# One hybrid block in float32 precision: topk rounds, score evictions and filler matmuls of the first mixer put in another order

## What is computed

```
proj = h @ w_in[l]
(c_q, k_a, v_a, k_idx, w_idx, q_b, k_b, v_b, gate_a, gate_b) = jnp.split(proj, offsets, axis=-1)
...
y_a = dsa_attention(q_a, k_a, v_a, q_idx, k_idx, w_idx, w_uv_a[l], top_k)      # 128 best keys by an index score
y_b = stick_breaking_attention(q_b, k_b, v_b)                                  # 8 heads of 64, causal
merged = jax.nn.sigmoid(gate_a) * (y_a @ w_o_a[l]) + jax.nn.sigmoid(gate_b) * (y_b @ w_o_b[l])
x = x + merged @ w_out[l]
```

## Time and profile before

| | us |
|---|---|
| median of 3 runs | 1981.68 (1981.31 to 1981.76) |
| the profiled execution | 1981.31 |
| its span, first to last instruction | 1979.4 |
| TensorE busy | 1901.5 (96%) |
| VectorE busy | 1044.2 (53%) |
| ScalarE busy | 699.4 (35%) |
| mean granted clock | 0.992 |

### The profile page before, as it was taken

One profiled execution on the slowest core, in us unless ns is written; L12 is line 12 of the kernel. 1 busy time (PEld: TensorE's weight loads), 2 busy tenths in 40 slices (PEclk: granted clock), 3 DMA queues, 4 the chain that ended last, 5 costly groups with the idle time before them and its releaser, 6 DMA issues.

```text
span 1979.4 us, 21957 instructions
## 1 busy us (share of the span) xinstructions
PE 1901.5 (96%) x8807; PEld 1373.9 (69%) x8807; DVE 1044.2 (53%) x1690; ACT 699.4 (35%) x1139; POOL 42.0 (2%) x67
## 2 busy tenths in 40 slices
PE   7999999998999989999999999999999999999998
PEld 6888888875888757888888878877676444443443
DVE  5443554457887886544334447566765333332333
ACT  5321232335655364333222234565642111111111
POOL 0000000100000001000000000000001000000000
PEclk9999999999999999999999999999999999999999
DMA  6323334125333304333333323222169999999997
GB/s 174 101 88 99 103 96 107 52 76 62 81 84 63 103 22 149 91 94 100 89 106 96 96 86 98 73 64 64 58 246 374 421 420 420 420 421 420 420 421 286
DMA packets 256302, 338.65 MB, mean 171 GB/s; under 512 B 10001, under 2 KB 218897, under 8 KB 232641
## 3 DMA queue, kind: packets, MB, share of 16 engines
q1 hardware_dynamic: 249744, 320.71, 47.2%
q0 software_dynamic: 5872, 15.41, 2.2%
q10 hardware_dynamic: 576, 1.05, 0.1%
HBM read 332.74 MB, written 8.39 MB: 172 GB/s over the span
## 4 chain that ended last, share of the span: by engine, by line
PE 71%; DMA 11%; DVE 10%; ACT 6%; issue 2%; SPq 0%; DVEq 0%; ACTq 0%
PE bank L183 70%; DMA large<-w_up 10%; PE bank L186 1%; ACT wH L189 1%; ACT T L189 1%; ACT p L189 1%; DVE PTL L195 1%; DVE y L195 1%; DVE p L198 1%; DVE score L201 0%; ACT SPH L189 0%; DVE st L207 0%; DVE gt L195 0%; DVE stage4L L195 0%; DMA gates<-gt 0%
## 5 line engine op out<-in xcount | busy, mean ns | idle before, releaser
L183 PE MATMUL bank<-hH,wH 128*128 128x512 f32 x1096 | 432.6, 395 | 12.4 <-DVE stage0L L195 11.7
L183 PE MATMUL bank<-hL,wH 128*128 128x512 f32 x1096 | 427.3, 390 | 0.0
L189 ACT ACTIVATE wH<-stage 128x1024 fp32r<-128x1024 f32 (+3 forms) x231 | 228.5, 999 | 98.3 <-PE bank L183 84.0
L183 PE MATMUL bank<-large,xF 128*64 128x512 f32 x1024 | 237.8, 607 | 17.2 <-DMA large<-w_up 15.1
L183 PEld LDWEIGHTS bank<-hH,wH 128*128 128x128 f32 x1096 | 206.3, 188 | 58.0 <-DVE stage0L L195 11.7
L183 PEld LDWEIGHTS bank<-hL,wH 128*128 128x128 f32 x1096 | 206.3, 188 | 43.5 <-issue 1.7
L183 PEld LDWEIGHTS bank<-large,xF 128*64 128x64 f32 x1024 | 75.6, 139 | 149.6 <-issue 142.2
L183 PE MATMUL bank<-hidH,wH 128*128 128x512 f32 x352 | 137.4, 390 | 2.1 <-DVE stage2L L195 0.9
L183 PE MATMUL bank<-hidL,wH 128*128 128x512 f32 x352 | 136.9, 389 | 0.0
L195 DVE TENSOR_TENSOR yoL<-bank,yoH 64x512 fp32r<-64x512 f32 x64 | 44.1, 689 | 148.7 <-ACT yoH L189 147.7
L183 PE MATMUL bank<-large,hF 128*64 128x512 f32 x512 | 116.0, 595 | 0.0
(11 more groups left out here) (494 smaller groups left out, 3339.6 us busy)
## 6 DMA issues: line engine op xcount, KB each, us to landing
large<-w_gate SPq DMA_DIRECT2D x64, 1024.0 KB, 27.0
large<-w_up SPq DMA_DIRECT2D x64, 1024.0 KB, 26.7
large<-w_down SPq DMA_DIRECT2D x64, 1024.0 KB, 26.7
stage<-w_in SPq DMA_DIRECT2D x56, 512.0 KB, 4.1
stage<-w_gate SPq DMA_DIRECT2D x44, 512.0 KB, 3.8
stage<-w_up SPq DMA_DIRECT2D x44, 512.0 KB, 3.8
stage<-w_down SPq DMA_DIRECT2D x16, 512.0 KB, 3.5
stage<-w_out SPq DMA_DIRECT2D x12, 512.0 KB, 3.9
```

The lines of the kernel that those rows point to most:

```text
L183: return self.e.matmul(*a, **k) if self.e is not None else Nothing()
L189: return self.e.activation(*a, **k) if self.e is not None else Nothing()
```

## The change

It does four things.

1. In the list of steps, rounds of `topk` stand at other places within the same section between two even `b1`, the number per section being the same. In the section before `b1(0)` two rounds are now ahead of the evictions of the pair's projections. Before `b1(2)` two rounds and a third are ahead of the evictions and of `b1_split(1)`, with a fourth behind that. Before `b1(4)` the eviction of `gate(7)` waits for a later `evict()`, two rounds stand ahead of `b1_max(3)`, and `b1_split(3)` is behind the evictions. Before `b1(6)` `b3(4)` and its eviction are earlier, and a round stands ahead of the evictions.
2. `b1` of an even head waits for the remainder of both halves of the keys (`kb_even` and `kb_oddL`) and no longer for the even half alone.
3. Filler matmuls: 9 ahead of `b1(0)`, 7 ahead of `b1(2)`, 9 ahead of `b1(6)`, and 13 where there were 6 ahead of `expand(0)`.
4. `values(0)` stands behind `logits(4)` and the eviction of a gate.

```diff
-                left.append(Step("split_qk", ..., y=gts.take(("qk_odd", c) if which else ("qk", c)), ...
+                left.append(Step("split_qk", ..., y=gts.take(("qk", c, which)), ...
...
             score(3, 1, low4)
+            topk(1)
             qk(0, 1, 7)
+            topk(1)
             evict()
+            topk(1)
+            gate(5)
             topk(2)
-            gate(5)
-            topk(3)
             b1(0)
...
             qk(3, 0, 6)
+            b3(4)
             qk(3, 1, 7)
+            b3_split(4)
             part("b1_max", 5)
...
-            values(0)
             logits(4)
             evict()
+            values(0)
             topk(2)
             expand(0)
...
-                        keep_clock(s.banks[0], {0: 6}.get(n, 0))
+                        keep_clock(s.banks[0], {0: 13}.get(n, 0))
...
                     elif s.kind == "b1":
+                        keep_clock(s.z[0], {0: 9, 2: 7, 6: 9}.get(n, 0))
                         pe.wait_ge(*after("kb_zero", n % 2))
-                        pe.wait_ge(*after("qk_odd" if n % 2 else "qk_even", n // 2))
-                        pe.wait_ge(*after("qk", n // 2))
+                        pe.wait_ge(*after("qk", n // 2, 1))
...
-                            low(M.qb[1][:, :], s.y.t[:, :], M.qb[0][:, :], 0.125).then_inc(*did("qk", n))
+                            low(M.qb[1][:, :], s.y.t[:, :], M.qb[0][:, :], 0.125).then_inc(*did("qk", n, 0))
...
-                                low(M.kb[e][1][pp, :], s.y.t[pp, :], M.kb[e][0][pp, :]).then_inc(*did(("qk_even", "qk_odd")[e], n))
+                                t = low(M.kb[e][1][pp, :], s.y.t[pp, :], M.kb[e][0][pp, :])
+                            t.then_inc(*did("qk", n, 1))
```

More of the change, by code:

```diff
@@ L546, in qk @@
                 b = dense(steps, ("qk", c, which), wcols("w_in", (520, 1032)[which] + c * 128, 128), 8, h, ("qkf", c, which), None, n)
-                left.append(Step("split_qk", n=c, k=which, bank=b, y=gts.take(("qk_odd", c) if which else ("qk", c)), held=("mm", "b1", 2 * c - 1) if c else ("sc", 3, 7)))
+                left.append(Step("split_qk", n=c, k=which, bank=b, y=gts.take(("qk", c, which)), held=("mm", "b1", 2 * c - 1) if c else ("sc", 3, 7)))
             def vb_rows(kk):
@@ L679, in mixer1 @@
             part("b1_max", 1)
+            topk(2)
+            evict()
             topk(1)
             part("b1_split", 1)
-            evict()
             b3(0)
+            topk(1)
+            qk(1, 1, 7)
             b3_split(0)
-            qk(1, 1, 7)
             evict()
             part("b2", 1)
-            topk(4)
+            topk(1)
             part("b2_exp", 1)
@@ L710, in mixer1 @@
             b3(2)
+            topk(2)
             part("b1_max", 3)
-            topk(1)
-            part("b1_split", 3)
             evict()
             b3_split(2)
+            part("b1_split", 3)
+            topk(1)
             qk(2, 1, 7)
+            part("b2", 3)
+            topk(1)
             evict()
-            part("b2", 3)
-            topk(3)
             part("b2_exp", 3)
@@ L744, in mixer1 @@
             part("b1_split", 5)
+            topk(1)
             evict()
-            b3(4)
-            b3_split(4)
             part("b2_exp", 5)
-            topk(2)
+            topk(1)
             part("b2_split", 5)
```

## The result

The kernel with the change took 1993.1 us (median of 5 runs, 1992.2 to 1994.95); the kernel before took 1981.76 on the same chip (1981.31 to 1985.2). The ratio is 1.0056, with a 95% interval of 1.0045 to 1.0068. The forecast was 1991.8, the direction slower. The profiled execution of after took 1993.76, with a span of 1991.9, so the span is 12.5 longer than before's 1979.4.

What follows compares the result with a forecast made beforehand. TensorE works nearly without a break, its even b1 mostly released by VectorE's kb_even, so work ahead of that counts. Terms 2.30 + 2.72 + 4.78 - 0.1 + 0.4 = 10.1 us gave 1991.8, range 1985.5 to 1995.5.

Steps and rivals of the forecast that it cites:

- b1(0): First even b1: starts at 500.83 against 498.39, 2.44 us late, 1.72 for two rounds and 0.72 for the wait.
- small slack of 0.14: At b2(0), which had waited 0.14 us for VectorE: lateness behind it is 2.44 - 0.14 = 2.30 us.
- b2(1) and b1(2): Second section: b2(1) newly waits 1.5 us for T1L; b1(2) starts at 539.10, 5.02 us late, 2.72 more.
- b1(4): Third section: 3.8 us wait for bank 7, covered by later keys on VectorE; start 581.26, 9.80 late, 4.78 more.
- the rival in which the clock falls: Clock falls in the unfilled holes at qk(2,1) and b1(4), 1.5 us longer or more: 1993.3 to 1994.8, chance 0.16.
- a sign of being wrong: PEclk below 1 between 560 and 585 with b1(4) at its forecast start; then the time is higher.
- b1(6): Last even b1: starts 1.44 us later on kb_oddL, held clock gives back 1.5; sum -0.1, start near 620.9.
- expand(0): Starts at about 687.0 against 684.43, mostly former idle; transposes at 687.8, fillers remove the half-speed stretch; +0.4 us.
- The sum: All five terms, b1(0) to expand(0): 10.1 us, nothing behind gives it back; time 1991.8.
- part of the delay is not on the path: Moved rounds fit VectorE's 3.40 us hole, b1(4) term about half, 2.4 less, b2(1)'s 1.5 absorbed: 1988, chance 0.12.
- absorbed later: Expert stage streams weights; if its start did not hang on PE, all would end as before, 1982; chance 0.05.
- Faster by the clock: Fillers keep the clock full from b1(6) and expand(0) on, VectorE waits do not grow: 1978.5, chance 0.05.

Runs made afterwards that it cites:

- first section alone: Kernel before with only the first section's topk rounds moved, two ahead of the evictions of the first pair: 1987.25 us, ratio 1.0019.
- wait alone: Kernel before with one change, b1 of an even head waiting for the remainder of both halves of the keys: 1987.99 us, ratio 1.0029.
- gate 7's eviction back: Kernel after with the eviction of gate 7 put back to behind b2(2), everything else as after: 1993.66 us, ratio 1.0048.
- second profile of before: Kernel before, unchanged, profiled a second time: 1984.11 us in one run, beside 1984.33 for before.
- the kernel with the edits at expand: Kernel before with values(0) behind logits(4) and the gate's eviction, and 13 fillers ahead of expand(0): 1982.38 us in one run, beside 1983.13 for before.
- the fillers alone: Kernel before with only the filler matmuls, 9, 7 and 9 ahead of b1(0), b1(2), b1(6) and 13 for 6 ahead of expand(0): 1984.85 us, ratio 1.0015.
- third section alone: Kernel before with only the third section's order, gate 7's later eviction and the moved rounds, neither the wait nor fillers: 1987.79 us, ratio 1.0018.
- gate 7 late alone: Kernel before with only the eviction of gate 7 made late, no topk round moved: 1988.09 us, ratio 1.0027.
- the one without fillers: Kernel after without its new fillers, none at b1 and 6 at expand(0), orders and waits as after: 2000.03 us, ratio 1.0078.
- the one with the fine wait: Kernel after with b1 of an even head released again by kb_even and not by both halves: 1991.12 us, ratio 1.0044.
- the kernel with the repair: Kernel before with VectorE's weight remainder moved behind kb_oddL, and ybL made while ACT rounds the keys: 1977.24 us, ratio 0.9973.

## Why the prediction held, step by step

The times of after here are less the 0.6 us that it was late at 484.

- **b1(0): right.** 501.42 - 0.6 = 500.8 against 500.83. The two parts are confirmed apart: two rounds 1.72 on VectorE (first section alone), the other half of the keys 0.7 (wait alone). b2(0) followed the dense step by 0.22, so the small slack of 0.14 was used up as said.
- **b2(1) and b1(2): right in the profile after; this section was not run alone.** The new wait for `T1L` is 1.27 (forecast 1.5). b1(2) is at 538.87 against 539.10.
- **b1(4): right in place, 0.2 low.** The wait for bank 7 is 3.87 (3.8), b1(4) at 581.46 against 581.26. The wait on `kb_oddL` is 0.16, where I had said over 2: because the clock fell in the hole in front, b2(3) ended only just ahead of the keys. The step that failed is the one that had b1(4) late because of VectorE alone. Two rows of VectorE in after show how near it was:

```profile
579.23 0.69 DVE L195 TENSOR_TENSOR gt<-bank,rn 128x512 f32<-128x512 f32 x1 [0.31 <-PE bank L183]
...
581.32 0.69 DVE L195 TENSOR_TENSOR kb_oddL<-gt,kb_oddH 64x512 fp32r<-64x512 f32 x1
```

  The keys' eviction, forecast with VectorE as its last, waited 0.31 for TensorE's dense step, which ran at half speed. This is the rival in which the clock falls, in the first of the two holes, the one that I had called covered. It was covered but for that 0.3. The second did not come. By the rule of the Trainium skill weighed ahead (TensorE: Matmul & The Clock Gate, "Why this matters for your kernels") this hole should cost clock, and after's granted clock of 0.50 from 570 to 576 agrees.

  So two routes to b1(4) met within half a microsecond. VectorE's alone is about 4.7 by the runs (4.1 with gate 7's eviction back, and 0.6 for that eviction), against the forecast 4.78. TensorE's is about 5.0: 3.87 of hole less the 1.24 that it idled at b1(4) before, and what is then left of the 5.21, 2.4 for the half-speed matmuls and 0.16 of wait. That the second came out so near the first is luck; the forecast had not reckoned it. The prediction also named a sign of being wrong, a PEclk below 1 between 560 and 585 with b1(4) at its forecast start. That sign came, at 569 to 577.
- **b1(6): in place, with the clock held.** Its start is 621.0 against 620.9, and it ran at full speed. From b1(4) to the step behind b1(6) it is 41.98 against 42.09 before, the forecast -0.1. The section was not run alone, and the reason was shaky, so this is in part luck: the second profile of before and the kernel with the edits at expand show that the 1.5 us it gives back were not lost in every execution of before.
- **expand(0): right at first, then overrun by the clock.** 696.5 against 696.7 that the forecast gives (687.0 and the 9.7 of lateness ahead of this term), transposes 10.3 late net. But a half-speed stretch came at 706. At the `expand` behind the first the lateness was 10.5 (703.15 against 692.62), 10 us later it was 11.0 (713.83 against 702.84), as at the merge: what the fillers had gained was lost again.
- **The sum.** The merge is 11.0 late, 10.4 net; forecast 10.1. The lateness is still there at the end, as said. The other 1.4 us arose behind `haH`, where the change does nothing. From `haH` to the end, the kernels here took between 514.3 and 518.0 us in no order that follows the edits. TensorE's waits there differ between the two profiles: 2.3 for `ge` against 0.6, 16.8 for the transfers of `w_up` against 15.1, none for `a32r` against 1.0, and the half-speed loss is 9.3 against 10.2. Together that is about 1.5 more, an estimate. The 2.2 to 2.3 at `ge` also stand in six other kernels here and not in the rest, so I put it down to the spread; what decides it is not shown. So the median of 1993.1 is 1.3 above the forecast's 1991.8 for reasons that lie mostly outside the forecast sum: 0.6 ahead of the section, 0.3 in it and 1.4 behind it, less 0.7 by which the profiled execution was above the median and the 0.4 that the forecast had allowed for this.

The rival "part of the delay is not on the path" is out by gate 7's eviction back in its place (4.1, with VectorE as the last at b1(4), where that rival has 2.4) and by the full 1.27 at b2(1); "absorbed later" is out by `haH`. "Faster by the clock" is out, and the fillers alone show why: even with no half-speed loss in this section the merge was 0.6 later.

## What to carry to other kernels

Count only what stands ahead of the last instruction on which the bottleneck engine hangs: a round ahead of the eviction cost its full time, one behind it next to nothing. Follow every route to that instruction: two delays on different routes did not add up (4.6 and 4.1 made 5.2), and removing one left the other. Put filler matmuls only into holes that are there whatever you do; they then bought up to 8 us, while those that lengthened a hole cost at least as much as they saved. And before a half-speed stretch is charged to a hole, profile the same program twice.

## What the runs showed of the hardware

- An idle of 1.93 to 1.95 us ahead of b1(6) was followed by a granted clock of 0.50 in both profiles of before and in the kernels with the first section alone, the third section alone and gate 7 late alone, but not in those with the coarse wait alone and with the edits at expand. With the coarse wait alone, an idle of 1.97 stood at b1(2) and at b1(4), and only the second was followed by it. The idle of 3.9 us was followed by it in all five kernels that have it (after, the one without fillers, the one with the fine wait, the third section alone, gate 7 late alone, where it was 4.3).
- A fall that is taken away can turn up elsewhere: the kernel with the repair lost its clock at the merge, at a place where before's first profile had kept it and its second had not. The medians therefore move less than the starts of one profile.
- Nine 128x512 fillers run from 498.34 to 500.55, about 0.25 us each, and hold the clock across a hole of 3 us without delaying what follows (b1(0) at 501.42 with them, 501.35 without).
